# Between a gating layer and a latent-attention layer: how the next norm's sum of squares is formed, and which engine does which piece

## The chip, the core and the metric

The kernel runs on one core of a Trainium2 chip. The metric is the device time of one execution in microseconds (us). Every time inside a profile is counted from the start of the core's span.

## The reference, cut to what matters

Two residual layers and a third block follow one another, for one sequence of 256 tokens with 2048 channels, in float32. Around the change this is computed:

```
x = x + gate * rms_norm(y, post_g)                 # end of layer 0, y = (u * vm * silu(z)) @ sgu_w_out
h = rms_norm(x, pre_g) * (1 + scale) + shift       # start of layer 1 (latent attention)
z = h @ mla_w_in                                   # 2048 -> 3072, first block: 512 columns
rms_norm(a, g) = a * rsqrt(mean(a * a) + 1e-6) * g
```

`gate`, `scale` and `shift` are vectors of 2048 numbers for each layer, made from the condition `c` and the weights `ada_w`. Each norm needs a sum over all 2048 channels of a token before any channel can go on, so at this place the end of one matrix product, two norms in a row and the beginning of the next matrix product form one dependent chain.

## The kernel before, in words

**Tiles.** The 256 tokens are two tiles of 128 (t = 0 and 1), tokens on partitions. Channels are handled in four blocks of 512 (b = 0 to 3) and in eight pairs of 128-channel columns (p = 0 to 7). `x[:, t, :]` is the residual stream, `y[:, t, :]` the output of the mixer and later the normalized input of the next layer.

**Matrix products in three parts.** Each weight and each activation is split into a rounded high part and a low part, and TensorE runs high x high, high x low and low x high. A weight chunk is 128 x 1024 numbers (two groups of 128 input channels by 512 output columns). For every chunk ScalarE makes the high part (`hi_next`, L616 to L631, the copy at L630), VectorE the low part (`lo_next`, the subtraction at L1305), and TensorE uses both. `AHEAD` is 3: the engines make chunk q + 3 at step q, in four slots (`CHUNKS`). `act_steps(n, k)` and `dve_steps(n, k)` are k such steps. A slot comes free when TensorE has used it for both tiles, at `chunk_used`. SyncE loads the raw weights into four slots of two chunks each and waits only for the low part of a chunk four loads back.

**Order.** Every engine has one queue in an order written out by hand; semaphores tie the queues together. Nothing is scheduled at run time, so an instruction that waits holds everything behind it on its engine.

**End of layer 0.** The last product (`sgu_w_out`, second half of its input channels) runs in four blocks. In blocks 0 to 2 TensorE fills a PSUM bank, ScalarE copies it to `stage`, GpSimd adds it to `y`, ScalarE squares `y` with an accumulated sum (`bss`, L959), and GpSimd multiplies `y` by the gate vector `grow` (`gate`, L2302, signals `y_gated`). Beside this VectorE makes weighted sums of `ada_w` (`ada_sum`, L1330) for layer 1. The last four chunks of block 3 are run tile by tile (`pe_by_tiles`, L2543, L2544, L2547): first tile 0 for four chunks (`half_done`), then eight small matmuls (`columns`, L2481), then tile 1.

**The transition, per tile.** ScalarE squares the last block out of PSUM (`act_tile_square`, L770). VectorE adds the four block sums (`dve_tile_ss`, L1484, L1485), multiplies the last block by the gate (`dve_tile_gated`, L1498), ScalarE takes the root (`act_tile_root`, L763), VectorE the reciprocal (`dve_tile_rstd`, L1490). VectorE updates `x` in four blocks (`dve_x_update`, L1503), ScalarE squares each updated block (`act_x_square`, L777), the sums give a second root and reciprocal, and VectorE writes the normalized blocks of `x` to `y` (`dve_x_normal`, L1509), which releases TensorE's transposes.

**Pairs.** `pe_pair` (L2570) transposes a pair of 128-channel columns into one of four PSUM banks. `act_pair` scales and shifts both with the modulation (L791, "modulates") and rounds the result to `a_hi` (L798, "rounds"). `dve_pair` subtracts for `a_lo` (L1533, the "low part" of an activation pair). Pairs 0 to 3 are the first half of the channels of tile 0, pairs 4 to 7 that of tile 1, pairs 8 to 15 the second half of both, tile by tile. In the kernel before, VectorE modulates pairs 2 and 3 (`dve_modulated`, L1517) and ScalarE only rounds them.

**Start of layer 1.** The first block of `mla_w_in` has eight chunks, called M0 to M7 here. M0 to M3 are run for tile 0 and then again for tile 1; tile 0's M0 needs the low part of pair 0, M1 that of pair 1, and so on; tile 1's M0 to M3 need pairs 4 to 7. M4 to M7 are run for both tiles at once and need pairs 8 to 15, two each. Around the first four transposes TensorE has matmuls whose result is not read (`unread`, L2608): six in front of them and five behind.

## Time and profile before

| | |
|---|---|
| median of 3 runs | 2481.65 us (2478.64 to 2482.20) |
| the profiled execution | 2477.93 us |
| its span on the core | 2476.1 us (1.8 us of it lie outside the span) |
| granted TensorE clock, mean | 0.999 of full speed |
| TensorE matmul (PE) busy | 2433.2 us, 98% |
| VectorE (DVE) busy | 1889.0 us, 76% |
| ScalarE (ACT) busy | 1399.4 us, 57% |
| GpSimd (POOL) busy | 442.0 us, 18% |
| instructions | 31108 |

PEld is the weight load of TensorE, which overlaps the matmuls. A row of the timeline gives the start and the length of an instruction or of a merged group, and in brackets how long the engine had sat idle before it and who released it. Lengths include the tail of an instruction: the next one on the same engine can start about 0.08 us before the printed end.

### The profile page before, as it was taken

How to read it: one execution, taken by the hardware profiler on the slowest of the kernel's cores; microseconds unless marked ns; L12 is line 12 of the kernel's file. 1: busy time of each engine (PE TensorE's matmuls, PEld its weight loads, DVE VectorE, ACT ScalarE, POOL GpSimd, SP SyncE). 2: the span in 40 equal slices, each digit the busy share in tenths (PEclk: the TensorE clock that was granted, in tenths of full speed). 3: DMA queues.
4: the chain of work that ended last, by engine and by line, in shares of the span. 5: the costliest groups of instructions: out<-in, count | busy, mean ns of one | idle time of the engine just before them, and what ended most of it. 6: DMA issues, size and time to landing. Idle time of an engine off the chain costs nothing.

```text
span 2476.1 us, 31108 instructions
## 1 busy us (share of the span) xinstructions
PE 2433.2 (98%) x11597; PEld 2018.7 (82%) x11597; DVE 1889.0 (76%) x2295; ACT 1399.4 (57%) x1934; POOL 442.0 (18%) x298
## 2 busy tenths in 40 slices
PE   6999999999999999998999999999999999999999
PEld 5888888888887989887888888888888888888887
DVE  7899798977777787866655555557988878788884
ACT  6655765444447555555566676755655545555553
POOL 0264563111020000110000000043111021111111
PEclk9999999999999999999999999999999999999999
DMA  9999677978784877754555556455465555646454
GB/s 364 321 341 349 237 256 273 336 283 290 271 313 149 246 212 220 233 208 149 167 173 163 177 153 183 157 187 187 155 236 170 204 187 191 217 170 221 170 203 154
DMA packets 370999, 549.47 MB, mean 222 GB/s; under 512 B 31405, under 2 KB 158129, under 8 KB 370225
## 3 DMA queue, kind: packets, MB, share of 16 engines
q1 hardware_dynamic: 368688, 539.54, 64.6%
q10 hardware_dynamic: 1824, 6.04, 0.7%
q0 software_dynamic: 352, 2.11, 0.2%
q8 instruction: 83, 1.36, 0.2%
q14 instruction: 52, 0.42, 0.0%
HBM read 545.53 MB, written 2.11 MB: 221 GB/s over the span
## 4 chain that ended last, share of the span: by engine, by line
PE 88%; DVE 8%; ACT 2%; issue 1%; DMA 1%; SPq 0%; POOL 0%; DVEq 0%; ACTq 0%; POOLq 0%
PE ps L2393 48%; PE ps L2398 24%; DVE lo L1305 3%; PE ps L2423 2%; PE ps L2419 2%; PE ps L2420 2%; DVE ps L1330 1%; PE ps L2379 1%; PE ps L2378 1%; PE ps L2380 1%; DVE lo L1282 1%; DMA raw<-in_sgu_w_in 1%; PE ps L3007 1%; PE ps L2655 1%; ACT hi L630 1%
## 5 line engine op out<-in xcount | busy, mean ns | idle before, releaser
L1305 DVE TENSOR_TENSOR lo<-raw,hi 128x1024 fp32r<-128x1024 f32 x550 | 706.9, 1304 | 350.8 <-ACT hi L630 350.2
L630 ACT ACTIVATE hi<-raw 128x1024 fp32r<-128x1024 f32 x550 | 571.3, 1051 | 431.3 <-PE ps L2398 352.7
L2393 PE MATMUL ps<-hi,a_hi 128*128 128x512 f32 (+1 forms) x2016 | 798.6, 396 | 2.1 <-issue 0.9
L2393 PE MATMUL ps<-hi,a_lo 128*128 128x512 f32 (+1 forms) x2016 | 785.6, 390 | 0.0
L2398 PE MATMUL ps<-lo,a_hi 128*128 128x512 f32 (+1 forms) x2016 | 539.0, 389 | 1.5 <-DVE lo L1305 1.5
L616 ACT ACTIVATE hi<-raw 128x1024 fp32r<-128x1024 f32 x339 | 358.2, 1060 | 292.7 <-PE ps L2398 255.2
L1282 DVE TENSOR_TENSOR lo<-raw,hi 128x1024 fp32r<-128x1024 f32 x339 | 424.4, 1272 | 107.2 <-ACT hi L616 105.0
L2393 PEld LDWEIGHTS ps<-hi,a_hi 128*128 128x128 f32 x2016 | 378.7, 188 | 85.1 <-issue 5.3
L2398 PEld LDWEIGHTS ps<-lo,a_hi 128*128 128x128 f32 x2016 | 378.4, 188 | 81.1 <-DVE lo L1305 1.9
L2393 PEld LDWEIGHTS ps<-hi,a_lo 128*128 128x128 f32 x2016 | 378.9, 188 | 74.4
L2393 PE MATMUL ps<-hi,b_hi 128*128 128x512 f32 x880 | 347.4, 395 | 0.6 <-ACT y L1015 0.3
L2393 PE MATMUL ps<-hi,b_lo 128*128 128x512 f32 x880 | 343.2, 390 | 0.0
L2398 PE MATMUL ps<-lo,b_hi 128*128 128x512 f32 x880 | 235.7, 390 | 0.0
L2227 POOL TENSOR_TENSOR v<-v,stage 128x512 f32<-128x512 f32 (+1 forms) x88 | 146.5, 1665 | 395.8 <-ACT stage L649 371.8
L2398 PEld LDWEIGHTS ps<-lo,b_hi 128*128 128x128 f32 x880 | 165.2, 188 | 35.2
L2393 PEld LDWEIGHTS ps<-hi,b_hi 128*128 128x128 f32 x880 | 165.3, 188 | 34.6 <-issue 0.7
L2393 PEld LDWEIGHTS ps<-hi,b_lo 128*128 128x128 f32 x880 | 165.4, 188 | 33.2
L2227 POOL TENSOR_TENSOR v<-v 128x512 f32<-128x512 f32 x48 | 79.2, 1662 | 589.1 <-ACT v L809 304.7
L1330 DVE SCALAR_TENSOR_TENSOR ps<-raw,cond,ps 128x512 f32<-128x512 f32 x194 | 137.6, 747 | 0.9 <-DMA raw<-in_ada_w 0.8
L2227 POOL TENSOR_TENSOR x<-x,stage 128x512 f32 (+1 forms) x38 | 71.2, 1874 | 332.5 <-DVE stage L1548 310.6
L649 ACT ACTIVATE stage<-ps 128x512 f32<-128x512 f32 x120 | 65.3, 593 | 51.4 <-PE ps L2398 48.2
L1330 DVE SCALAR_TENSOR_TENSOR acc_b<-raw,cond,acc_b 128x512 f32<-128x512 f32 x90 | 72.8, 809 | 0.0
(351 smaller groups left out, 2436.6 us busy)
## 6 DMA issues: line engine op xcount, KB each, us to landing
raw<-in_sgu_w_in SPq DMA_DIRECT2D x88, 1024.0 KB
raw<-in_ada_w SPq DMA_DIRECT2D x64, 1024.0 KB
raw<-in_w_up SPq DMA_DIRECT2D x64, 1024.0 KB
raw<-in_w_down SPq DMA_DIRECT2D x64, 1024.0 KB
raw<-in_w_in SPq DMA_DIRECT2D x42, 1024.0 KB
raw<-in_ada_w SPq DMA_DIRECT2D x64, 512.0 KB
raw<-in_sgu_w_out SPq DMA_DIRECT2D x32, 1024.0 KB
raw<-in_w_in SPq DMA_DIRECT2D x128, 256.0 KB
```

The lines of the kernel that those rows point to most:

```text
L616: nc.scalar.activation(by_rows(hi[:, q % CHUNKS, :]), raw_piece(place), ACT.Copy).then_inc(hi_ready, 1)
L630: nc.scalar.activation(hi[:, q % CHUNKS, 0:width], raw[:, r % RAWS, q % 2 * CW:q % 2 * CW + width], ACT.Copy).then_inc(hi_ready, 1)
L649: nc.scalar.activation(to, ps[:, 2 * s + t, 0:width], func, scale=rstd[:, t:t + 1] if normed else 1.0).then_inc(acc_free, 1)
L1282: nc.vector.tensor_tensor(by_rows(lo[:, q % CHUNKS, :]), raw_piece(place), by_rows(hi[:, q % CHUNKS, :]).bitcast(F32), ALU.subtract).then_ ...
L1305: nc.vector.tensor_tensor(lo[:, q % CHUNKS, 0:width], raw[:, r % RAWS, q % 2 * CW:q % 2 * CW + width], hi[:, q % CHUNKS, 0:width].bitcast( ...
L1330: ins = nc.vector.scalar_tensor_tensor(out=out[:, :] if a == j == 3 else to, in0=w, scalar=c, in1=to, op0=ALU.mult, op1=ALU.add)
L2227: return nc.gpsimd.tensor_tensor(out_, a, b, op)
L2393: nc.tensor.matmul(ps[:, 2 * s + t, 0:width], x[:, k0 + j, t * P:(t + 1) * P], hi[:, c, w], start=begins, stop=False)
L2398: ins = nc.tensor.matmul(ps[:, 2 * s + t, 0:width], x2[0][:, k0 + j, t * P:(t + 1) * P], lo[:, c, w], start=False, stop=last and j == kts - 1)
L2419: nc.tensor.matmul(ps[:, bank, :], left(j)[0], hi[:, c, w], start=begins and j == 0, stop=False)
L2420: nc.tensor.matmul(ps[:, bank, :], left(j)[1], hi[:, c, w], start=False, stop=False)
L2423: ins = nc.tensor.matmul(ps[:, bank, :], left(j)[0], lo[:, c, w], start=False, stop=ends and j == 1)
```

## The change

The sum of squares of the updated `x` is no longer taken from the updated `x`. With r the factor of the gated norm (`rgate`), the new x is x + r*y, so its sum of squares is the old sum + r * (the sum of 2*x*y) + r * r * (the sum of y*y), y being gated. ScalarE sums the squares of gated `y` (`gx[..., 0, b]`) and VectorE the products 2*x*y (`gx[..., 1, b]`), block by block: those of blocks 0 to 2 are placed inside the last product, those of block 3 in the transition. `dve_tile_next` then forms the sum in four small dependent operations, without waiting for the updates of `x`.

In the transition ScalarE normalizes the first two blocks of each tile (`act_x_normal`) and modulates all pairs; VectorE updates two blocks of each tile before the second reciprocal or beside it, and the other four just ahead of pair 4's low part. ScalarE's roundings of the weight chunks and VectorE's low parts stand at other places between them. TensorE's six unread matmuls in front of the transposes are gone; the five behind them stay. The squares of `x` (`act_x_square`) and VectorE's modulation of pairs 2 and 3 are gone here.

The diff, with the declarations of the new buffers and semaphores left out:

```diff
@@ -777,6 +783,26 @@
+        def act_x_normal(act, n, t, b, updated):
+            at = slice(b * NB, (b + 1) * NB)
+            act.wait_ge(n_rstd, n.nrm.base)
+            act.wait_ge(x_updated, updated)
+            nc.scalar.activation(y[:, t, at], x[:, t, at], ACT.Copy, scale=rstd[:, t:t + 1]).then_inc(n_out, 1)
+        def act_gated_square(act, t, b):
+            nc.scalar.activation(gated_parts[:, 2 * b + t, :], y[:, t, b * NB:(b + 1) * NB], ACT.Square,
+                                 accum_out=gx[:, t, 0, b:b + 1]).then_inc(gated_sq, 1)
+        def act_block_gated(act, layer, b):
+            act.wait_ge(y_gated, 6 * layer + 2 * b + 2)
+            if layer:
+                act.wait_ge(gated_sq, 8)
+            for t in range(T):
+                act_gated_square(act, t, b)
@@ -959,35 +985,39 @@
...
                     n.bsq.base += 1
+                if b:
+                    act_block_gated(act, 0, b - 1)
             act_steps(act, n, 2)
             nc.scalar.activation(early[:, :], ones[:, :], ACT.Sqrt)
             act_steps(act, n, 1)
+            act_block_gated(act, 0, 2)
             act.wait_ge(stage_free, n.stg.at(2))
             act.wait_ge(half_done, 1)
             act_tile_square(act, n, 0, 1)
             act_tile_root(act, n, 0)
+            act.wait_ge(acc_free, n.acc.base + 4)
+            act_gated_square(act, 0, 3)
+            act_tile_root(act, n, 0)
+            act_x_normal(act, n, 0, 0, 1)
+            act_x_normal(act, n, 0, 1, 2)
             act_steps(act, n, 1)
-            for b in range(4):
-                act_x_square(act, n, 0, b, b + 1)
+            act.wait_ge(scales, GROUPS + 1)
+            act_pair(act, n, 0, *PAIRS[0], 1)
             act.wait_ge(chunk_used, n.chunk.base + 2 + CHUNKS)
             act_tile_square(act, n, 1, 1)
+            act_tile_root(act, n, 1)
+            act_pair(act, n, 1, *PAIRS[1], 1)
+            act.wait_ge(acc_free, n.acc.base + 6)
+            act_gated_square(act, 1, 3)
             n.acc.base += 2
-            act_tile_root(act, n, 0)
             act_steps(act, n, 1)
+            act_pair(act, n, 2, *PAIRS[2], 1)
             act_tile_root(act, n, 1)
-            act.wait_ge(scales, GROUPS + 1)
-            act_pair(act, n, 0, *PAIRS[0], 1)
-            act_pair(act, n, 1, *PAIRS[1], 1)
-            act_x_square(act, n, 1, 0, 5)
-            act_steps(act, n, 1)
-            act_x_square(act, n, 1, 1, 6)
-            act_pair(act, n, 2, *PAIRS[2], 1, rounds_only=True)
-            act_pair(act, n, 3, *PAIRS[3], 1, rounds_only=True)
-            act_x_square(act, n, 1, 2, 7)
-            act_x_square(act, n, 1, 3, 8)
-            act_steps(act, n, 1)
-            act_tile_root(act, n, 1)
+            act_x_normal(act, n, 1, 0, 3)
+            act_x_normal(act, n, 1, 1, 4)
+            act_pair(act, n, 3, *PAIRS[3], 1)
+            act_steps(act, n, 2)
             for i in range(4, 16):
                 act_pair(act, n, i, *PAIRS[i], 1)
                 if i in (7, 9, 11, 13):
@@ -1484,12 +1514,36 @@
-        def dve_tile_rstd(dve, n, t):
+        def dve_tile_rstd(dve, n, t, to=rstd):
             dve.wait_ge(n_sd, n.nrm.base + 1)
-            nc.vector.reciprocal(rstd[:, t:t + 1], sd[:, t:t + 1]).then_inc(n_rstd, 1)
+            nc.vector.reciprocal(to[:, t:t + 1], sd[:, t:t + 1]).then_inc(n_rstd, 1)
             n.nrm.base += 1
             dve.wait_ge(n_rstd, n.nrm.base)
+        def dve_crossed(dve, t, b):
+            at = slice(b * NB, (b + 1) * NB)
+            nc.vector.scalar_tensor_tensor(out=crossed_parts[:, 2 * b + t, :], in0=x[:, t, at], scalar=2.0, in1=y[:, t, at],
+                                           op0=ALU.mult, op1=ALU.mult, accum_out=gx[:, t, 1, b:b + 1]).then_inc(x_crossed, 1)
+        def dve_block_crossed(dve, layer, b):
+            dve.wait_ge(y_gated, 6 * layer + 2 * b + 2)
+            for t in range(T):
+                dve_crossed(dve, t, b)
+        def dve_tile_next(dve, n, layer, t):
+            one = slice(t, t + 1)
+            dve.wait_ge(x_crossed, 8 * layer + 7 + t)
+            dve.wait_ge(gated_sq, 8 * layer + 7 + t)
+            then(dve, n, nc.vector.tensor_reduce(gsum[:, t, :], gx[:, t, :, :], AX, ALU.add))
+            then(dve, n, nc.vector.scalar_tensor_tensor(out=cross[:, one], in0=gsum[:, t, 0:1], scalar=rgate[:, one], in1=gsum[:, t, 1:2],
+                                                        op0=ALU.mult, op1=ALU.add))
+            then(dve, n, nc.vector.scalar_tensor_tensor(out=xsq[:, one], in0=cross[:, one], scalar=rgate[:, one], in1=xsq[:, one],
+                                                        op0=ALU.mult, op1=ALU.add))
+            nc.vector.tensor_scalar(var[:, one], xsq[:, one], D * EPS, 1.0 / D, ALU.max, ALU.mult).then_inc(n_var, 1)
         def dve_tile_gated(dve, layer, t, s, frees):
@@ -1497,14 +1551,16 @@
             dve.wait_ge(gate_landed, 16 * (layer + 1))
             nc.vector.tensor_tensor(y[:, t, last], ps[:, 2 * s + t, :], grow[:, last], ALU.mult).then_inc(acc_free, frees)
-        def dve_x_update(dve, t, b):
+        def dve_x_update(dve, t, b, factor=rstd):
             at = slice(b * NB, (b + 1) * NB)
-            nc.vector.scalar_tensor_tensor(out=x[:, t, at], in0=y[:, t, at], scalar=rstd[:, t:t + 1], in1=x[:, t, at],
+            nc.vector.scalar_tensor_tensor(out=x[:, t, at], in0=y[:, t, at], scalar=factor[:, t:t + 1], in1=x[:, t, at],
                                            op0=ALU.mult, op1=ALU.add).then_inc(x_updated, 1)
-        def dve_x_normal(dve, t, b):
+        def dve_x_normal(dve, t, b, updated=None):
+            if updated is not None:
+                dve.wait_ge(x_updated, updated)
             at = slice(b * NB, (b + 1) * NB)
             nc.vector.tensor_scalar(y[:, t, at], x[:, t, at], rstd[:, t:t + 1], None, ALU.mult).then_inc(n_out, 1)
@@ -1751,12 +1807,17 @@
                 n.acc.base += 2
                 if b == 1:
                     ada_part(dve, n, 10)
+                if b:
+                    dve_block_crossed(dve, 0, b - 1)
+                else:
+                    then(dve, n, nc.vector.tensor_scalar(xsq[:, :], ss[:, :], D * EPS, None, ALU.add))
             ada_cols(dve, n, 1, 0, 7, 7, 0)
             for k in range(5):
                 lo_next(dve, n)
                 if k in (0, 2):
                     ada_sum(dve, n, 2 + k // 2)
                 n.chunk.base += 1
+            dve_block_crossed(dve, 0, 2)
             ada_keep(dve, n, 1, 28)
...
@@ -1767,50 +1828,42 @@
             dve.wait_ge(block_sq, 2 + n.bsq.base)
             dve_tile_ss(dve, n, 0, bss)
             dve_tile_gated(dve, 0, 0, 1, 2)
+            dve_tile_rstd(dve, n, 0, rgate)
+            dve.wait_ge(acc_free, n.acc.base + 4)
+            dve_crossed(dve, 0, 3)
+            dve_tile_next(dve, n, 0, 0)
+            dve_x_update(dve, 0, 0, rgate)
+            dve_x_update(dve, 0, 1, rgate)
             dve_tile_rstd(dve, n, 0)
-            dve.wait_ge(y_gated, 6)
-            for b in range(4):
-                if b == 3:
-                    dve.wait_ge(acc_free, n.acc.base + 4)
-                dve_x_update(dve, 0, b)
             dve_steps(dve, n, 1)
-            n.sq.base += 4
-            dve.wait_ge(n_ss, n.sq.base)
-            dve_tile_ss(dve, n, 0, xss)
             n.bsq.base += 1
             dve.wait_ge(block_sq, 2 + n.bsq.base)
-            dve_tile_rstd(dve, n, 0)
-            for b in range(2):
-                dve_x_normal(dve, 0, b)
             dve_tile_ss(dve, n, 1, bss)
             dve_tile_gated(dve, 0, 1, 1, 2)
+            dve_pair(dve, n, 0, *PAIRS[0], 1)
+            dve_tile_rstd(dve, n, 1, rgate)
+            dve.wait_ge(acc_free, n.acc.base + 6)
+            dve_crossed(dve, 1, 3)
+            dve_pair(dve, n, 1, *PAIRS[1], 1)
+            dve_steps(dve, n, 1)
+            dve_tile_next(dve, n, 0, 1)
+            dve_x_update(dve, 1, 0, rgate)
+            dve_pair(dve, n, 2, *PAIRS[2], 1)
             dve_tile_rstd(dve, n, 1)
-            dve_x_update(dve, 1, 0)
-            dve_pair(dve, n, 0, *PAIRS[0], 1)
-            dve_x_update(dve, 1, 1)
-            dve_modulated(dve, n, 2, *PAIRS[2], 1, 1)
-            dve_pair(dve, n, 1, *PAIRS[1], 1)
-            dve_modulated(dve, n, 3, *PAIRS[3], 1, 1)
-            dve_steps(dve, n, 1)
-            dve_x_update(dve, 1, 2)
-            dve.wait_ge(acc_free, n.acc.base + 6)
-            dve_x_update(dve, 1, 3)
-            dve_pair(dve, n, 2, *PAIRS[2], 1)
+            dve_x_update(dve, 1, 1, rgate)
             dve_steps(dve, n, 1)
             dve_pair(dve, n, 3, *PAIRS[3], 1)
             n.kept.base += 16
             n.acc.base += 2
             dve_steps(dve, n, 1)
-            n.sq.base += 4
-            dve.wait_ge(n_ss, n.sq.base)
-            dve_tile_ss(dve, n, 1, xss)
-            dve_tile_rstd(dve, n, 1)
-            dve_x_normal(dve, *PIECES[2])
-            dve_x_normal(dve, *PIECES[3])
+            dve_x_update(dve, 0, 2, rgate)
+            dve_x_update(dve, 1, 2, rgate)
+            dve_x_update(dve, 0, 3, rgate)
+            dve_x_update(dve, 1, 3, rgate)
             for i in range(4, 16):
                 dve_pair(dve, n, i, *PAIRS[i], 1)
                 if i in (4, 5, 6, 7):
-                    dve_x_normal(dve, *PIECES[i])
+                    dve_x_normal(dve, *PIECES[i], i + 1)
                 if i in (9, 11, 13):
                     dve_steps(dve, n, 1)
@@ -2685,17 +2738,15 @@
             block_in(0, {3: lambda: pe_ada_parts(pe, n, 4, 7, 7, 0, 11)})
             for c in range(4):
                 pe_chunk(pe, n, A, 1, 2 * c, 2, NB, False, False)
-            pe_by_tiles(pe, n, A, 1, range(8, 16, 2), ends=True, tells=True, before={(1, 0): columns})
-            n.acc.base += 2
             kept0 = n.kept.base
             split0 = n.tg.base
             normal = lambda t, p: 2 + PIECES.index((t, p // 2)) + 1
             pair = lambda i: pe_pair(pe, n, i, *PAIRS[i], normal(*PAIRS[i]), t_kept, kept0)
             split = lambda i: pe.wait_ge(t_lo, split0 + i + 1)
             n.kept.base += 16
+            pe_by_tiles(pe, n, A, 1, range(8, 16, 2), ends=True, tells=True, before={(1, 0): columns})
+            n.acc.base += 2
             pe.wait_ge(acc_free, n.acc.at())
-            unread(0, 6)
             for i in range(4):
                 pair(i)
             unread(0, 5)
```

## Rows read from the trace of the kernel before

**Rows 1.** The page, part 1: busy time and share of the span.

```profile
PE 2433.2 (98%) x11597; PEld 2018.7 (82%) x11597; DVE 1889.0 (76%) x2295; ACT 1399.4 (57%) x1934; POOL 442.0 (18%) x298
```

**Rows 2.** Windows: length, busy (count) of PE, PEld, DVE, ACT, POOL, granted clock, DMA.

```profile
722.00:744.00 22.00, 22.00 (x100) 18.22 (x99) 17.66 (x21) 10.77 (x15) 7.69 (x5) 1.00 0.81 286
764.00:801.00 37.00, 31.79 (x156) 24.16 (x155) 26.24 (x53) 30.38 (x70) 0.00 (x0) 1.00 0.28 78
```

**Rows 3.** Timeline of TensorE: start, length, what, [idle before, released by].

```profile
764.44 1.50 PE L2608 MATMUL ps<-cst 128*128 128x128 f32 x12
766.26 1.09 PE L2570 MATMUL ps<-cst,y 128*128 128x128 f32 x8 [0.32 <-DVE y L1509]
767.19 1.28 PE L2608 MATMUL ps<-cst 128*128 128x128 f32 x10
768.74 0.50 PE L2543 MATMUL ps<-hi,a_hi 128*128 128x512 f32 x1 [0.27 <-DVE a_lo L1533]
...
773.81 0.50 PE L2543 MATMUL ps<-hi,a_hi 128*128 128x512 f32 x1 [0.93 <-DVE a_lo L1533]
...
777.70 0.41 PE L2570 MATMUL ps<-cst,y 128*128 128x128 f32 x2 [2.02 <-issue]
...
779.92 0.50 PE L2543 MATMUL ps<-hi,a_hi 128*128 128x512 f32 x1 [0.19 <-DVE a_lo L1533]
...
800.57 0.36 PE L2393 MATMUL ps<-hi,a_hi 128*128 128x448 f32 x1
```

**Rows 4.** Timeline of VectorE, same columns.

```profile
743.05 1.23 DVE L1305 TENSOR_TENSOR lo<-raw,hi 128x1024 fp32r<-128x1024 f32 x1 [1.73 <-ACT hi L630]
...
759.07 0.16 DVE L1346 COPY mod<-ps 128x4 f32<-128x4 f32 x1 [1.88 <-PE ps L2481]
...
759.85 0.69 DVE L1498 TENSOR_TENSOR y<-ps,v 128x512 f32<-128x512 f32 x1
...
760.64 2.74 DVE L1503 SCALAR_TENSOR_TENSOR x<-y,rstd,x 128x512 f32<-128x512 f32 x4
...
768.26 0.42 DVE L1533 TENSOR_TENSOR a_lo<-tf,a_hi 128x256 fp32r<-128x256 f32 x1
...
773.34 0.42 DVE L1533 TENSOR_TENSOR a_lo<-tf,a_hi 128x256 fp32r<-128x256 f32 x1
...
779.44 0.43 DVE L1533 TENSOR_TENSOR a_lo<-tf,a_hi 128x256 fp32r<-128x256 f32 x1 [1.44 <-ACT a_hi L798]
```

**Rows 5.** Timeline of ScalarE, same columns.

```profile
758.33 0.60 ACT L770 ACTIVATE acc_b<-ps 128x512 bf16<-128x512 f32 x1 [5.05 <-PE ps L2547]
...
760.61 1.06 ACT L630 ACTIVATE hi<-raw 128x1024 fp32r<-128x1024 f32 x1 [0.46 <-PE ps L2547]
...
767.00 0.79 ACT L791 ACTIVATE tf<-ps,mod,hscale 128x128 f32<-128x128 f32 x2
767.82 0.42 ACT L798 ACTIVATE a_hi<-tf 128x256 fp32r<-128x256 f32 x1
...
769.90 1.04 ACT L630 ACTIVATE hi<-raw 128x1024 fp32r<-128x1024 f32 x1
```

**Rows 6.** Groups by line, 757 to 801 us: busy, mean ns of one, idle before.

```profile
L1305 DVE TENSOR_TENSOR lo<-raw,hi 128x1024 fp32r<-128x1024 f32 x12 | 14.4, 1219 | 0.0
L649 ACT ACTIVATE v<-ps 128x512 f32<-128x512 f32 x1 | 0.6, 597 | 0.7 <-PE ps L2398 0.7
L777 ACT ACTIVATION_READ_ACCUMULATOR acc_b<-x 128x1 f32 x8 | 1.5, 186 | 0.0
L763 ACT ACTIVATE sd<-var 128x1 f32<-128x1 f32 x4 | 0.8, 200 | 3.0 <-DVE var L1485 3.0
L1485 DVE TENSOR_SCALAR var<-ss 128x1 f32<-128x1 f32 x4 | 0.6, 154 | 0.1
```

**Rows 7.** Windows at the next transition, columns as in rows 2.

```profile
1124.70:1127.76 3.06, 1.10 (x9) 0.86 (x8) 2.49 (x11) 2.44 (x8) 0.00 (x0) 1.00 0.00 0
1127.76:1134.58 6.82, 3.53 (x17) 3.46 (x17) 6.75 (x18) 6.15 (x16) 0.00 (x0) 0.50 0.02 3
```

More of the change, by code:

```diff
@@ L314, in build @@
         xss = sb("xss", [P, T, 4])
+        gx = sb("gx", [P, T, 2, 4])
+        gsum = sb("gsum", [P, T, 2])
+        xsq, rgate, cross = (sb(k, [P, T]) for k in ("xsq", "rgate", "cross"))
         early = sb("early", [P, 1])
@@ L371, in build @@
         turned_x = tf[:, :, :].rearrange("p a (b e s) -> p (a b) e s", b=2, e=2)
+        gated_parts = v[:, 0, D:2 * D].bitcast(BF16).rearrange("p (k n) -> p k n", k=8)
+        crossed_parts = v[:, 1, :].rearrange("p (k n) -> p k n", k=8)
         junk = stage[:, :, :].rearrange("p t n -> p (t n)").bitcast(BF16)
@@ L417, in build @@
         block_sq, gate_kept, y_gated = sem("block_sq"), sem("gate_kept"), sem("y_gated")
+        gated_sq, x_crossed = sem("gated_sq"), sem("x_crossed")
         gate_written, gate_landed = sem("gate_written"), sem("gate_landed")
```

## The prediction

> **What bounds the kernel now.** I read the page's busy shares first: TensorE is busy 98% of the span [rows 1], so time can only be won or lost where TensorE stands idle or does work that nobody needs. Then the windows. In the last product of layer 0 TensorE is busy in all of 22 us; in the transition, 764 to 801 us, it is busy 31.8 of 37, some of that with unread matmuls, while ScalarE is busy 30.4 [rows 2]. Here the order of ScalarE's and VectorE's queues sets the time. TensorE's timeline shows the holes one by one [rows 3]: unread matmuls from 764.44, transposes at 766.26, the first real chunk (M0, tile 0) at 768.74, M2 at 773.81 after 0.93 us idle, pair 4's transposes at 777.70 after 2.02 us idle, tile 1's M0 at 779.92, and the next block at 800.57. From 764.44 that is 36.1 us. Nothing else of the kernel is touched, and behind this stage TensorE is the bound again, so the shift of 800.57 is the shift of the whole time, if nothing gives it back.
>
> **How the sum is made.** I walk through the three queues in their new order. An instruction starts when the one before it lets go, or when what it waits for has come, plus 0.05 to 0.1 us. Lengths: product, update of 512 columns 0.75 each and 0.67 from start to start (four take 2.74 us) [rows 4]; weight chunk's low part 1.22 [rows 6], 1.14 from start to start; its rounding on ScalarE 1.05, 0.96 from start to start; modulate and round one pair 0.79 + 0.42, in all 1.15 until ScalarE is free [rows 5]; square 0.60 [rows 5] plus 0.19 to read the accumulator, overlapping to 0.7; copy of 512 columns 0.60, root 0.20, a small VectorE operation 0.15, 0.19 when the next depends on it [rows 6]; pair's low part 0.42, gate product 0.69 [rows 4]. The old order walked in the same way reaches the next block 0.2 us later than the trace, so I trust differences to some 0.5 us.
>
> **Inside the last product.** Twelve instructions are new: six squares on ScalarE (0.7 us each), six products on VectorE. I cost them at nothing. Those of blocks 0 and 1 fall beside idle time such as the 1.73 us in front of VectorE's low part at 743.05 [rows 4]. The products of block 2 come at 757.2, where VectorE sits idle 1.88 us until 759.07 [rows 4], and the squares into ScalarE's 5.05 idle us before 758.33 [rows 5]. If that cover were gone, tile 0's chain would start later by the excess.
>
> **The product with an accumulated sum** is in no row of VectorE. Lower bound: the update, the same operation and shape without the sum, 0.75 [rows 4]. Upper bound: the nearest longer row, 1.22, a low part of twice the columns [rows 6]. I take 0.94: the update plus ScalarE's 0.19 for reading an accumulator, the nearest row to that step [rows 6]. Walked with 0.75 the shift of the end is 3.3 us, with 0.94 3.5, with 1.22 4.1. The Trainium skill (Vector Engine (DVE) Microarchitecture Reference, section 7, Points that are easy to get wrong) says that this instruction with two SBUF sources other than bf16 runs at half throughput, with no port left for reading the accumulator. The update without the sum, two f32 sources, takes 0.75 [rows 4]; no row here has the sum with it, so the trace can't bear the rule out. By it the product would take twice the update, about 1.4 us, and the shift would be 4.6.
>
> **Tile 0's chain.** Unchanged up to the gate product, which ends at 760.54 [rows 4]. Then product to 761.6, four small operations to 762.4, root, and meanwhile two updates to 763.6; reciprocal to 763.8; ScalarE normalizes block 0 from 763.9 to 764.5. The old chain released the transposes at 766.26; now they start at 764.5, and the six unread matmuls (1.50 us [rows 3]) are gone. That is 1.7 us won. But ScalarE now has behind it: normalize block 1 to 765.0, round M0 (old at 760.61 [rows 5]) to 766.0, modulate and round pair 0 to 767.1, where the old one ended at 768.24. VectorE can't take pair 0's low part yet: tile 1's sum and gate product stand ahead of it, and they wait for ScalarE's square of tile 1 (767.0 to 767.7). So the low part starts at 768.65 (old: 768.26 [rows 4]) and M0 at 769.1 against 768.74. **The win is spent: +0.4.**
>
> **Tile 1's chain.** ScalarE: pair 1 to 769.5, square of gated y to 770.1, round M1 to 771.2. VectorE's low part of M1 ends at 772.4, about as before. Then four small operations to 773.0, update to 773.7, pair 2's low part from 773.7 (old 773.34), reciprocal to 774.2. TensorE could start M2 at 774.1. But M2's rounding, old at 769.90 [rows 5], now stands behind two normalizations (774.2 to 775.6, the second waiting for its update) and pair 3 (to 776.7): it ends at 777.7. **TensorE starts M2 at 777.8 against 773.81 [rows 3]: +4.0, after some 4.8 us idle.** That is what is late next.
>
> **What comes back, and goes again.** The old 2.02 us in front of pair 4 go, since block 0 of tile 1 is normalized by then: M3 starts only 1.5 us late. But VectorE has behind M2: its low part to 779.0, pair 3's, M3's low part to 780.4, and then four updates, 2.7 us, all in front of pair 4's low part, which starts at 783.1 against 779.44 [rows 4]. Tile 1's M0 starts at 783.5 against 779.92 [rows 3], or against 780.08 in the walk of the old order: **+3.5.** From there both orders alternate pair by pair in the same way, ScalarE giving the pace, and the shift stays to the end of the block: 804.1 against 800.57. No DMA is added, and the DMA engines are busy 0.28 of this stage [rows 2], so I add nothing for loads.
>
> On the profiled execution's own 2477.93 us (span 2476.1) this gives 2481.4. That execution stands 3.7 us under the median of 2481.65; on the median I forecast 2481.65 + 3.5 = **2485.2 us**. A measurement of this kernel can tell about 0.2%, 5.0 us, from no change, so this is a forecast of "within 0.2%", on the slow side.
>
> **Rival 1, slower by more than 0.2%: the clock falls in the new hole.** At the next transition TensorE was busy 1.10 us of 3.06, and then the granted clock went from 1.00 to 0.50 (2.4 to 1.2 GHz) for 6.82 us [rows 7]. In the old transition at 764 it stayed at 1.00 [rows 2], but there the longest hole was 2.02 us, and now there are 4.8 us before M2 and 2.4 before tile 1's M0. Against: a fall in the first hole costs nothing if the clock is back by 783, since TensorE waits there for VectorE anyway. It decides if low clock still holds when tile 1's chunks begin. Slowing TensorE's pieces by 1.85 in the walk for 3.4 to 6.8 us from 779 to 784 adds 0.7 to 2.1 us; with 2.1 the time is 2487.3, +0.23%. The Trainium skill (TensorE: Matmul & The Clock Gate, What's actually happening) says that the default is the throttled clock and that activity releases it, which agrees with rows 7.
>
> **Rival 2: the accumulated product is dear** (the upper bound and above): 2485.7 to 2486.3, a wait of VectorE in tile 0's chain.
>
> **Rival 3: TensorE isn't held at M2.** If the 4.8 us don't appear (ScalarE reaches M2's rounding by 774, through a quicker chain than the rows give), the four updates ahead of pair 4 are left and the walk ends 2.1 us after the old one (2483.8); with them overlapped too it is 0.2 (2481.9). If the 1.7 us won at the transposes and the 2.02 us at pair 4 stayed won in full, it would be 2478. For it: both really are released earlier. Against: seven pieces of ScalarE, each with a row, stand in front of M2's rounding. That the change doesn't do what its title says is part of the forecast: the four updates stand in one lump in front of pair 4's low part, so the low parts aren't even there.
>
> **Chances.** Forecast as walked 0.54; rival 1 0.18; rival 2 0.10; rival 3 0.18. Slower by over 0.2% gets most of rival 1, a third of rival 2 and, since medians of three vary by 1 to 2 us, some 0.10 of the forecast: 0.27. Faster by over 0.2% needs 2476.7: a third of rival 3 at most, 0.06. The rest, 0.67, is within 0.2%. The range takes in rival 1 with noise above (2488.8) and most of rival 3 below (2479.5).
>
> **What would show it.** Right: transposes at about 764.5; M0 near 769; one hole of 4 to 5 us before M2, released by ScalarE's L630; no hole at pair 4; four updates in a row before pair 4's low part; a hole of about 2.4 us before tile 1's M0; next block at about 804; products of 0.75 to 0.94 us. Wrong: M2 starting before 775, a granted clock of 0.5 inside 765 to 800, products of 1.2 us or more, or waits for DMA in the block.

## The result, and the profile after

The changed kernel takes 2483.41 us (median of 22 runs, 2481.24 to 2487.49) against 2481.57 for the kernel before on the same chip (22 runs): the ratio is 1.0012, 95% interval 1.0006 to 1.0017. By the ratio it is slower by 3.0 us (1.5 to 4.2); the two medians themselves differ by 1.84 us. Either is within the 0.2% that counted as no change. The profiled execution took 2483.45 us, span 2481.6. TensorE's share is the same as in [rows 1]. Part 1 of the page:

```profile
PE 2435.2 (98%) x11585; PEld 2019.5 (81%) x11585; DVE 1891.1 (76%) x2308; ACT 1403.0 (57%) x1942; POOL 441.9 (18%) x298
```

The two spans differ by 5.5 us, more than the ratio says: the profiled execution of the kernel before, 2477.93 us, was faster than each of its 22 runs (lowest 2478.64). To see where, I measure one stage in every kernel of this study: from the start of the eight small matmuls that make the modulation of the layer (TensorE's last work before the gate of the last block can be applied) to the first 448-column matmul of the next block. Before, this **stage** goes from 758.08 to 800.57; after, from 759.85 to 806.01. So 1.77 us arise ahead of it, and **3.67 us in it**; nothing is left for the rest of the kernel. The stage is a steadier measure than the whole time: in the changed kernel and the six variants of it that keep the order up to there (experiments 1, 2, 3, 5, 9 and 10), tile 0's M0 starts 10.98 to 11.00 us into it. What does vary from one execution to the next is the clock, as experiment 12 shows. Windows over the stage and over the stretch with a low clock in it, columns as in [rows 2], before first:

```profile
758.08:800.57 42.49, 37.28 (x184) 28.81 (x183) 30.61 (x63) 34.33 (x79) 0.00 (x0) 1.00 0.33 97
```

The same of the kernel after:

```profile
759.85:806.01 46.16, 37.61 (x172) 28.92 (x171) 30.26 (x65) 34.76 (x75) 0.00 (x0) 0.93 0.30 92
777.00:783.83 6.83, 4.12 (x11) 3.27 (x12) 4.24 (x6) 4.24 (x8) 0.00 (x0) 0.52 0.24 78
```

No engine has noticeably more to do than before. TensorE stands idle 8.6 us of the stage (46.16 less 37.61), where it was 5.2. TensorE's timeline after shows where; it answers to [rows 3], with every start 1.8 us late from what came ahead of the stage:

```profile
766.32 1.18 PE L2623 MATMUL ps<-cst,y 128*128 128x128 f32 x8
767.34 1.28 PE L2661 MATMUL ps<-cst 128*128 128x128 f32 x10
...
770.84 0.50 PE L2596 MATMUL ps<-hi,a_hi 128*128 128x512 f32 x1 [2.22 <-DVE a_lo L1589]
...
779.71 0.77 PE L2596 MATMUL ps<-hi,a_hi 128*128 128x512 f32 x1 [4.88 <-ACT hi L636]
...
785.33 0.50 PE L2596 MATMUL ps<-hi,a_hi 128*128 128x512 f32 x1 [0.16 <-DVE a_lo L1589]
...
806.01 0.36 PE L2446 MATMUL ps<-hi,a_hi 128*128 128x448 f32 x1
```

M2 is at 779.71, behind a hole of 4.88 us that ScalarE's rounding ended. At pair 4 there is no hole any more. The granted clock was 0.50 from 777.2 to 784.1, so it fell inside the hole; in M2's own row the length is 0.77 where M0 took 0.50. VectorE's timeline, answering to [rows 4]:

```profile
758.90 0.69 DVE L1527 SCALAR_TENSOR_TENSOR v<-x,y 128x512 f32<-128x512 f32 x1
759.51 0.08 DVE L1527 DVE_READ_ACCUMULATOR v<-x,y 128x1 f32 x1
760.84 0.16 DVE L1376 COPY mod<-ps 128x4 f32<-128x4 f32 x1 [0.63 <-PE ps L2534]
...
763.37 0.22 DVE L1542 SCALAR_TENSOR_TENSOR cross<-gsum,rgate 128x1 f32<-128x1 f32 x1
...
770.37 0.41 DVE L1589 TENSOR_TENSOR a_lo<-tf,a_hi 128x256 fp32r<-128x256 f32 x1
...
779.59 1.23 DVE L1335 TENSOR_TENSOR lo<-raw,hi 128x1024 fp32r<-128x1024 f32 x1 [2.94 <-ACT hi L636]
...
782.21 2.73 DVE L1557 SCALAR_TENSOR_TENSOR x<-y,rgate,x 128x512 f32<-128x512 f32 x4
784.86 0.41 DVE L1589 TENSOR_TENSOR a_lo<-tf,a_hi 128x256 fp32r<-128x256 f32 x1
```

Pair 0's low part at 770.37 releases M0 at 770.84. VectorE sits idle 2.94 us for the same rounding as TensorE, and does its four updates in one lump after it; pair 4's low part comes at 784.86, and that releases tile 1's M0 at 785.33. ScalarE's timeline, answering to [rows 5]:

```profile
775.90 1.57 ACT L791 ACTIVATE y<-x,rstd 128x512 f32<-128x512 f32 x2 [0.86 <-DVE rstd L1520]
777.38 0.79 ACT L817 ACTIVATE tf<-ps,mod,hscale 128x128 f32<-128x128 f32 x2
...
778.52 1.99 ACT L636 ACTIVATE hi<-raw 128x1024 fp32r<-128x1024 f32 x2
```

These are tile 1's two normalizations, pair 3's modulation, and then the roundings of M2 and M3 back to back. The groups by line, 759 to 807 us, answer to [rows 6]:

```profile
L791 ACT ACTIVATE y<-x,rstd 128x512 f32<-128x512 f32 x4 | 2.8, 718 | 2.2 <-DVE rstd L1520 2.1
L1527 DVE SCALAR_TENSOR_TENSOR v<-x,y 128x512 f32<-128x512 f32 x4 | 2.7, 690 | 0.1
L1527 DVE DVE_READ_ACCUMULATOR v<-x,y 128x1 f32 x4 | 0.3, 84 | 0.0
```

The product with an accumulated sum takes 0.69 us and 0.08 for reading the accumulator; ScalarE's normalization takes 0.72.

### The profile page after: what moved, and what is told of

It reads as the page before. It is cut to its first block, busy times and chain, and to the rows that moved or that the text cites. A ratio compares the mean times of both kernels' runs of the same rounds, so it can differ in the third digit from the quotient of the medians.

```text
span 2481.6 us, 31102 instructions
## 1 busy us (share of the span) xinstructions
PE 2435.2 (98%) x11585; PEld 2019.5 (81%) x11585; DVE 1891.1 (76%) x2308; ACT 1403.0 (57%) x1942; POOL 441.9 (18%) x298
## 4 chain that ended last, share of the span: by engine, by line
PE 87%; DVE 7%; ACT 2%; issue 1%; DMA 1%; SPq 0%; POOL 0%; ACTq 0%; DVEq 0%; POOLq 0%
PE ps L2446 48%; PE ps L2451 24%; DVE lo L1335 2%; PE ps L2476 2%; PE ps L2473 2%; PE ps L2472 2%; DVE ps L1360 1%; DMA raw<-in_sgu_w_in 1%; PE ps L2432 1%; PE ps L2431 1%; PE ps L2433 1%; DVE lo L1312 1%; ACT hi L636 1%; PE ps L3058 1%; PE ps L2708 1%
```

## The experiments

**Theory A:** the order of two queues costs the 3.7 us. M2's rounding stands behind the normalizations and pair 3 on ScalarE, and four updates stand in a lump ahead of pair 4's low part on VectorE. **Rivals:** B, the twelve operations added inside the last product delay the stage; C, the clock that falls in the new hole costs it. Whole times scatter (31 runs of the kernel before on two other chips lie between 2478.7 and 2486.7 us), so the verdicts go by the stage, of one profiled execution each; each whole time stands with that of the kernel before on the same chip. Experiments 1 to 6, 9 and 10 have one run each, and so has the kernel before beside 1 to 4. To see what a move wins apart from a later fall of the clock, I also use the start of **tile 1's M0**, counted from the start of the stage: 21.84 us before the change, 25.48 after it. From there to the end of the stage it is 20.6 to 20.7 us in both, and in every variant with the old order behind it in which the clock holds from there on. In the runs' code the loops over pairs 4 to 15 are written out and the semaphore counts passed along; the extracts show what changes place.

**1. M2's rounding early.** Only one step of ScalarE moves:

```
 act_pair(act, n, 2, *PAIRS[2], 1)
+act_steps(act, n, 1)
 act_tile_root(act, n, 1)
...
 act_pair(act, n, 3, *PAIRS[3], 1)
-act_steps(act, n, 2)
+act_steps(act, n, 1)
```

> The changed kernel with one piece moved on ScalarE: the rounding of weight chunk M2 stands right behind pair 2 instead of behind the two normalizations of tile 1 and pair 3. Measure: the stage from the start of the eight small matmuls (ps<-ones,acc x8) to the first 448-column matmul, 42.49 us before the change and 46.16 after it. Theory A (the order of the two queues holds TensorE, first at M2's rounding, then at the four updates): M2 starts 3.6 to 3.9 us earlier, the hole of 4.88 us before it shrinks to about 1, but M3 waits for its own rounding, so the stage gets 1.5 us shorter, 44.7. Theory B (the added work and ScalarE's sum of work make the stage longer, whatever its order): the stage stays within 0.5 us of 46.16. Theory C (the low TensorE clock in the hole costs the time): the clock doesn't fall and the stage gets shorter by the 1.5 to 3 us that slow matmuls cost, whatever the updates do.

Measured: stage 45.30 us (763.00 to 808.30), whole 2485.76 against 2482.4. It wins 0.9 of the 3.7, less than A's 1.5. The clock was low twice, from 774.7 to 778.1 and from 788.3 to 791.7. The stage and the second low stretch, and tile 1's M0:

```profile
763.00:808.30 45.30, 38.72 (x172) 29.61 (x171) 30.21 (x65) 34.73 (x75) 0.00 (x0) 0.92 0.31 92
788.50:791.50 3.00, 3.00 (x10) 2.46 (x9) 0.82 (x2) 2.11 (x6) 0.00 (x0) 0.50 0.00 1
```

```profile
787.02 0.50 PE L2623 MATMUL ps<-hi,a_hi 128*128 128x512 f32 x1 [2.04 <-DVE a_lo L1603]
```

Tile 1's M0 is at 24.02 us (787.02 less 763.00), 1.46 earlier than in the changed kernel: that is A's 1.5. In the second low stretch, behind it, TensorE is busy all 3.00 us, so it is the bound there, and 0.6 us of the win are lost again.

**2. The updates spread.** Only VectorE's four updates move:

```
-dve_x_update(dve, 0, 2, rgate)
-dve_x_update(dve, 1, 2, rgate)
-dve_x_update(dve, 0, 3, rgate)
-dve_x_update(dve, 1, 3, rgate)
 dve_pair(dve, n, 4, *PAIRS[4], 1)
+dve_x_update(dve, 0, 2, rgate)
 dve_x_normal(dve, 0, 2, 5)
 dve_pair(dve, n, 5, *PAIRS[5], 1)
+dve_x_update(dve, 1, 2, rgate)
...
```

> The changed kernel with the four updates of x that stood in one lump in front of pair 4's low part now standing one by one behind the low parts of pairs 4, 5, 6 and 7, each just ahead of the normalization that needs it; ScalarE as in the changed kernel. Theory A: the hole before M2 stays at 4.9 us, pair 4's low part comes 1.8 us earlier or more, and the stage gets 1.8 us shorter, 44.4 us against 46.16. Theory B: within 0.5 us of 46.16. Theory C: the clock falls as in the changed kernel and the stage stays at 46.16.

Measured: stage 46.34 us, whole 2484.92 against 2482.4. By itself this is a miss for A. The stage's windows:

```profile
761.07:807.41 46.34, 39.16 (x171) 30.29 (x170) 30.54 (x65) 34.75 (x75) 0.00 (x0) 0.89 0.29 89
780.00:786.50 6.50, 5.58 (x14) 4.34 (x15) 3.63 (x5) 2.94 (x5) 0.00 (x0) 0.50 0.26 66
```

The clock was low from 779.9 to 786.7 here as well, but now pair 4's low part is early, and TensorE has chunks to do in that stretch: busy 5.58 of 6.50 us. Tile 1's M0 starts only when they are done, at 25.71 us (786.78 less 761.07), without a wait:

```profile
786.78 0.48 PE L2622 MATMUL ps<-hi,a_hi 128*128 128x512 f32 x1
```

Experiment 10 tests this reading.

**3. Both moves.** Edits 1 and 2 together.

> Both moves together: M2's rounding behind pair 2, and the updates spread. Theory A: 3.8 us shorter than the changed kernel, 42.3 us, which is what the stage took before the change (42.49), so the whole loss is these two places. Theory B: 45.7 us or more. Theory C: about 44 us, as with the first move alone.

Measured: whole 2481.70 against 2482.4, and the stage:

```profile
761.87:804.25 42.38, 37.33 (x172) 28.12 (x171) 30.58 (x65) 34.62 (x75) 0.00 (x0) 0.96 0.33 97
```

```profile
783.60 0.47 PE L2623 MATMUL ps<-hi,a_hi 128*128 128x512 f32 x1
```

42.38 us against 42.49 before the change, and tile 1's M0 is at 21.73 us (783.60 less 761.87) against 21.84. **The whole loss is back, by order alone**, with every added operation kept, though the clock was low in this run too, from 774.1 to 777.5, ahead of M2.

**4. The added operations alone.** The kernel before, with the squares and products inside the last product; nothing uses their sums:

```
 act_steps(act, n, 1)
+act_block_gated(act, 0, 2)
...
+dve_block_crossed(dve, 0, 2)
```

> The kernel before, with only the twelve added operations inside the last product (six squares of gated y on ScalarE, six products 2xy on VectorE); their sums are not used and the transition is the old one. Theory A: they are hidden; the three blocks in front take the same time as before (22.0 us for a block) and the stage is 42.5 us, within 0.2. Theory B: the block or the stage is longer by 1 us or more, since products of two SBUF tiles delay VectorE's low parts and tile 0's first sum.

Measured: stage 42.54 us, whole 2481.04 against 2482.4. Windows of the product and of the stage:

```profile
694.00:738.00 44.00, 44.00 (x196) 36.43 (x196) 37.83 (x41) 22.62 (x32) 12.21 (x8) 1.00 0.83 288
760.99:803.53 42.54, 37.32 (x183) 28.79 (x182) 30.93 (x65) 34.39 (x79) 0.00 (x0) 1.00 0.32 97
```

With the added work TensorE is busy in all of 44.00 us, though VectorE is busy in 37.83 of them. B falls.

**5. The hole filled.** Thirty unread matmuls ahead of M2, to hold the clock:

```
-(0, 2): lambda: (split(2),),
+(0, 2): lambda: (unread(1, 30), split(2),),
```

> The changed kernel with 30 matmuls of 128 columns whose result is not read, into a free PSUM bank, in TensorE's hole before M2, so that TensorE is not idle there. Theory A: the granted clock stays at 1.00 from 765 to 800 us, M2 and M3 run at full speed, but tile 1's M0 still waits for pair 4's low part behind the four updates: the stage stays at 46.2 us, within 0.3. Theory C (the low clock costs the time): the stage gets 1.5 us shorter or more.

Measured: stage 46.53 us (A said 46.2 within 0.3), whole 2486.04 against 2481.38. The clock had fallen at 774.2 already and was back at 777.6, ahead of the filling, so C wasn't tested as meant. But the run shows another thing, in TensorE's timeline and in the window over the filling:

```profile
777.79 6.86 PE L2687 MATMUL ps<-cst 128*128 128x128 f32 x60
784.41 0.47 PE L2622 MATMUL ps<-hi,a_hi 128*128 128x512 f32 x1
...
788.07 0.50 PE L2622 MATMUL ps<-hi,a_hi 128*128 128x512 f32 x1 [0.19 <-DVE a_lo L1602]
```

```profile
777.79:784.41 6.62, 6.62 (x61) 6.61 (x60) 3.65 (x6) 4.45 (x7) 0.00 (x0) 1.00 0.41 138
```

The filling, all of it at a clock of 1.00, is longer than the hole and holds M2 until 784.41. From the stage's start that is 2.4 us later than in the changed kernel, and the stage is only 0.37 us longer. Tile 1's M0 again waits for VectorE's low part; that came 0.4 us later since pair 4's transposes stand behind M2, and VectorE waited 0.34 us for ScalarE's rounding of the pair. So M2's own start isn't what sets the end: the rounding is, through VectorE, which waits for it ahead of the low parts and the four updates.

**6. The six unread matmuls.** The change took them out. Here the kernel before, without them:

```
-unread(0, 6)
```

> The kernel before with nothing changed but the six unread matmuls in front of the first transposes left out. Theory A: the transposes waited for the normalized x anyway (they were free at 765.94 and started at 766.26), so the stage stays at 42.5 us within 0.2, unless the clock falls. Rival: the six stood on the path and the stage gets up to 1.5 us shorter.

Measured: whole 2482.50 against 2481.38, and the stage:

```profile
761.46:805.08 43.62, 37.23 (x171) 28.40 (x170) 30.61 (x63) 34.32 (x79) 0.00 (x0) 0.96 0.31 95
782.30:785.50 3.20, 3.20 (x10) 2.45 (x9) 1.16 (x3) 1.67 (x5) 0.00 (x0) 0.50 0.56 214
```

```profile
781.07 0.41 PE L2570 MATMUL ps<-cst,y 128*128 128x128 f32 x2 [2.02 <-issue]
```

1.13 us longer than with them, all of it in a stretch with the clock low, 782.1 to 785.5, where TensorE is busy throughout. Up to pair 4's transposes nothing moved: they are at 19.61 us (781.07 less 761.46) against 19.62. So the six are off the path by themselves. Whether they hold the clock isn't shown: the fall came some 13 us behind the place where they stood, each kernel has one profile here, and experiment 12 shows a fall coming and going in one and the same kernel. The two executions with the six that have a profile, the kernel before and experiment 4, had none in the stage.

**7. The three queues reordered.** The changed arithmetic in a new order. ScalarE: two roundings (M0, M1) ahead of tile 0's root; M2's rounding right behind that root; block 1 of tile 0 normalized after pair 0; M3's rounding ahead of tile 1's normalizations. VectorE: low parts of M0 and M1 earlier, tile 0's updates 1 and 2 ahead of tile 1's gate, only one update left ahead of pair 4. TensorE: transposes of pairs 4 to 7 ahead of tile 0's M3. ScalarE's part of the diff:

```
+act_steps(act, n, 2)
...
-act_x_normal(act, n, 0, 0, 1)
-act_x_normal(act, n, 0, 1, 2)
+act_x_normal(act, 0, 0, 1, r0 + 2)
+act.wait_ge(chunk_used, m0 + 3 + CHUNKS)
+act_tile_square(act, n, 1, 1)
...
+act_x_normal(act, 0, 1, 2, r0 + 2)
...
-act_x_normal(act, n, 1, 0, 3)
-act_x_normal(act, n, 1, 1, 4)
...
+act_steps(act, n, 1)
+act_x_normal(act, 1, 0, 4, r0 + 4)
+act_x_normal(act, 1, 1, 5, r0 + 4)
```

> The changed kernel with the same pieces on the same engines, but ScalarE's, VectorE's and TensorE's queues of the transition in another order: the roundings of M0, M1 and M2 stand ahead of or between the first normalizations, tile 0's updates and low parts of weights fill VectorE's waits, the updates of blocks 2 and 3 are spread up to pair 7, and TensorE's transposes of pairs 5 to 15 stand one to three places earlier. Theory A, by the walk through the three queues: the stage takes 36.7 to 37.5 us against 46.16 after and 42.49 before, and the whole kernel is about 5 us faster than before (ratio 0.998) and 8 us faster than after. Theory B: no better than before, 42 us or more.

Measured: 2474.52 us (7 runs, 2471.8 to 2476.45) against 2481.38 (13 runs), ratio 0.9969 (0.9958 to 0.998). Its stage's window, and from the timeline the only two holes from the first transposes to the end of the stage:

```profile
758.03:794.46 36.43, 34.08 (x172) 27.40 (x170) 29.75 (x65) 34.02 (x75) 0.00 (x0) 1.00 0.38 114
```

```profile
765.14 0.63 PE L2649 MATMUL ps<-cst,y 128*128 128x128 f32 x4 [0.55 <-ACT y L791]
...
767.57 0.66 PE L2649 MATMUL ps<-cst,y 128*128 128x128 f32 x4 [1.80 <-ACT y L791]
```

The stage is 6.1 us shorter than before the change, and the whole 6.9 by medians. **This version beats both kernels:** its ratio to the kernel before is 0.9969, that of the changed kernel 1.0012.

**8. The same, normalized on VectorE.** Does it matter that ScalarE normalizes? The first two blocks of each tile go to VectorE, with the order adapted:

```
-act_x_normal(act, 0, 0, 1, r0 + 2)
-act_x_normal(act, 0, 1, 2, r0 + 2)
...
+dve_x_normal(dve, 0, 0, 1)
+dve_x_normal(dve, 0, 1, 2)
```

> As the reordered kernel, but VectorE writes the four first normalized blocks (0.48 us each, as before the change) and ScalarE does not; queues ordered anew for that. Theory A: by the walk the stage takes 37.1 to 37.9 us, about the same as with ScalarE normalizing, 5 us faster in all than before. A rival (what is saved on ScalarE pays twice, since ScalarE is the busiest engine of the stage): under 36.5 us.

Measured: 2474.87 us (7 runs), ratio 0.9969 (0.9958 to 0.998); stage 36.65. Not told apart from experiment 7: once the order fits, it makes no difference that these runs show which engine normalizes.

**9. and 10. The clock, by a pair.** The same filling in two kernels: 14 unread matmuls in place of five behind the first transposes, 19 ahead of M2. In 9 in the changed kernel, in 10 in the kernel of experiment 2:

```
-unread(0, 5)
+unread(0, 14)
...
-(0, 2): lambda: (split(2),),
+(0, 2): lambda: (unread(1, 19), split(2),),
```

> The changed kernel with TensorE kept busy: fourteen unread matmuls instead of five behind the first transposes (about 2.0 us more, the hole before M0 was 2.2), and nineteen before M2 (about 4.2 us; the hole was 4.9). The one with thirty before M2 was longer than its hole and came too late for a clock that had fallen at 774. Theory A: the granted clock stays at 1.00 through the stage and the stage takes 46.2 us, within 0.3, since VectorE's pair 4 is what tile 1 waits for and slow matmuls had room in front of it. Theory C (the low clock was part of the change's loss): 45.5 us or less.

> The same unread matmuls in the kernel with the updates spread, which took 46.34 us instead of the 44.4 walked, with a clock of 0.50 from 779.8 to 786.7 us. If the low clock ate the gain, the stage takes 44.2 to 44.7 us now, with a clock of 1.00. If spreading the updates is worth nothing (TensorE or ScalarE would have waited for something else), it stays at 46 us or more.

Measured: 9 has 2489.73 us and stage 47.13, 10 has 2481.28 us and stage 44.44, against 2481.14. Windows of 9, then of 10:

```profile
765.23:812.36 47.13, 43.37 (x228) 34.94 (x226) 30.13 (x65) 34.77 (x75) 0.00 (x0) 0.96 0.29 88
791.50:794.50 3.00, 3.00 (x10) 2.41 (x10) 0.30 (x1) 0.82 (x3) 0.00 (x0) 0.50 0.14 53
```

```profile
759.47:803.91 44.44, 42.04 (x228) 33.76 (x226) 30.55 (x65) 34.76 (x75) 0.00 (x0) 1.00 0.31 93
```

In 10 the clock held at 1.00, and the stage is 1.9 us shorter than in experiment 2 (46.34): the low clock was what hid A's gain there, and with it out of the way spreading the updates is worth 46.16 less 44.44, 1.7 us. Tile 1's M0 says the same, at 23.79 us (783.26 less 759.47) against 25.48 in the changed kernel and 25.71 in experiment 2:

```profile
783.26 0.50 PE L2622 MATMUL ps<-hi,a_hi 128*128 128x512 f32 x1 [0.21 <-DVE a_lo L1602]
```

In 9 the clock held through M2 and fell later (791.3 to 794.7), in a stretch where TensorE is busy throughout. Two rows of its TensorE timeline:

```profile
785.10 0.47 PE L2622 MATMUL ps<-hi,a_hi 128*128 128x512 f32 x1 [0.64 <-ACT hi L636]
...
790.73 0.50 PE L2622 MATMUL ps<-hi,a_hi 128*128 128x512 f32 x1 [1.90 <-DVE a_lo L1602]
```

From the stage's start these are M2 at 19.9 and tile 1's M0 at 25.5 us. In the changed kernel they are at 19.9 (779.71 less 759.85) and 25.5 too, with the clock low between them. So the fall at M2 cost it nothing up to there, and C falls for its profiled execution. The stage of 9 still got 1.0 us longer (A said 46.2 within 0.3): from tile 1's M0 to the end it took 21.6 us instead of 20.7, and the later fall lies there.

**11. The old arithmetic reordered.** What is the new sum worth, apart from the order? The kernel before with its queues rearranged in the manner of 7, ScalarE modulating every pair, the six unread matmuls gone; an extract:

```
-dve_modulated(dve, n, 2, *PAIRS[2], 1, 1)
...
-act_pair(act, n, 2, *PAIRS[2], 1, rounds_only=True)
+act_pair(act, n, 2, *PAIRS[2], 1)
```

> The kernel before with its own arithmetic (ScalarE squares the updated x, VectorE normalizes), only its three queues in an order found by the same walk, ScalarE modulating pairs 2 and 3, and the six unread matmuls gone. Walk: 38.2 us for the stage with 0.5 of error, against 42.49 before and 36.43 in the reordered kernel with the new sum of squares; as a whole about 4 us faster than before (ratio 0.998). Theory A: so the order alone is worth 4 us, and the new sum of squares 1 to 2 us more once the order lets it. Rival (the new sum is what makes the reordering possible): 41 us or more.

**12. Experiment 7 again,** beside it.

> The reordered kernel of e7 once more, on the same chip as e11, to compare the two: 36.4 us for the stage and a ratio to before of 0.9958 to 0.998; e11's ratio should lie 0.0005 to 0.001 above it.

Measured: 11 has 2476.27 us (9 runs), ratio 0.9979 (0.9969 to 0.9989), stage 39.84; 12 has 2476.46 us (10 runs), ratio 0.9975 (0.9965 to 0.9984), stage 37.89. The stages are 1.6 and 1.5 us longer than expected, with a clock fall in each. Windows of 11, then of 12:

```profile
760.62:800.46 39.84, 37.07 (x172) 29.68 (x170) 29.21 (x59) 35.32 (x83) 0.00 (x0) 0.91 0.34 105
```

```profile
760.25:798.14 37.89, 35.53 (x171) 28.84 (x170) 29.67 (x65) 34.14 (x75) 0.00 (x0) 0.95 0.35 109
770.50:773.50 3.00, 3.00 (x13) 2.81 (x13) 2.62 (x10) 2.92 (x9) 0.00 (x0) 0.50 0.40 153
```

12 is the kernel of 7, and its stage is 1.46 us longer. TensorE's busy time is 1.45 longer too (35.53 against 34.08), and the clock was low from 770.3 to 773.7, where 7 had none of it. That is the price of one fall on the path, in one and the same kernel. As whole times 11 and 12 aren't told apart; their stages differ by 1.95 us in favour of the new sum, with a clock fall in both, of 3.4 us in 12 and 6.8 in 11. What the new sum is worth by itself stays open, between nothing and about 2 us; most of the gain of either is order (in 11 with the six unread matmuls gone and ScalarE modulating every pair).

## Why the prediction was right

The forecast was +3.5 us and "within 0.2%, on the slow side". Measured are +3.67 in the stage, +3.0 (1.5 to 4.2) as a ratio of whole times, and 2483.41 us, inside the range. The forecast time itself, 2485.2, lies 1.8 us above that. Step by step, with 1.8 us taken off the times after for what came ahead of the stage:

- **Inside the last product: nothing.** Right. Experiment 4 has it alone: 42.54 against 42.49.
- **Transposes at 764.5.** Measured 764.5. **M0 at 769.1.** Measured 769.0. The win of 1.7 us at the transposes was spent in the places named.
- **M2 at 777.8 after a hole of 4.8 us.** Measured 777.9 and 4.88, ended by the rounding named.
- **The hole at pair 4 goes, four updates stand ahead of pair 4's low part at 783.1, tile 1's M0 at 783.5.** Measured 783.1 and 783.5. Experiment 3 shows that this lump and the late rounding are the whole loss.
- **Next block at 804.1.** Measured 804.2. From tile 1's M0 on it took 20.65 us before and 20.68 after, so the shift stayed as walked.
- **The product with the sum, 0.94.** Mis-sized: 0.69 + 0.08 = 0.77, close to its lower bound of 0.75. Rival 2 falls with it. The Trainium skill (Vector Engine (DVE) Microarchitecture Reference, section 7, Points that are easy to get wrong) has half throughput for two SBUF sources other than bf16. That isn't borne out: the 512 columns took 0.69 us, no longer than an update without the sum (four take 2.73), and no more for a column than a low part, also of two f32 sources in SBUF, with 1.23 for 1024.
- **ScalarE's normalization, 0.60.** Mis-sized: 0.72. The row I took it from reads PSUM and has no factor for each token, and this one reads SBUF and has one. The source alone doesn't make the difference: the squares of `x` in the kernel before (L777), out of SBUF without such a factor, took 0.62. The small operations of VectorE with two tensors took 0.22, not 0.15. These and the product's 0.17 too much went against each other in the walk, so part of the closeness at each station is luck.
- **A hole of 2.4 us before tile 1's M0.** Not there as idle time: 0.16 us. The clock had fallen at 777.2, in the hole before M2, and until 784.1 TensorE did M2 and M3 slowly, which filled the time in which it would have waited for VectorE anyway. In experiment 9, with the clock held, that hole is 1.90 us.

**Rival 1** was half right. Its mechanism came (the clock fell to 0.50 in the new hole), and with it one of my own signs of being wrong, a granted clock of 0.5 inside 765 to 800. Its condition, low clock while tile 1's chunks run, wasn't met in the profiled execution: the clock was back at 784.1, and tile 1's M0 started at 785.33. But I had it too narrow: I looked only for one fall at the largest hole. Experiments 1, 2, 3, 5, 6, 9, 11 and 12 show falls at several places of the stage. Some cost nothing that shows, as in experiment 3; those that a comparison could price where TensorE is the bound (1, 2, 6, 9, 12) cost 0.6 to 1.9 us. How much falls cost the changed kernel in its 22 runs isn't known, since only one execution has a profile. That low clock takes more of its runs is on record: the mean granted clock over a run is 0.996 to 0.998 in all 22 (0.997 in the profiled one), while the profiled execution of the kernel before had 0.999, and so had 11 of its 31 runs beside experiments 5 to 12, on other chips. **Rival 3** falls with the measured hole at M2. That the unread matmuls cost nothing to lose was my silent assumption; experiment 6 bears it out up to pair 4 and leaves open whether the fall behind it, 1.1 us, is theirs.

The 1.77 us ahead of the stage belong to no step. The stage starts between 758.0 and 765.2 us in the kernels of this study, with nearly the same work ahead; experiment 6, which has none of the added operations, starts at 761.46. In the two profiles, 0.43 us of the 1.77 arise before TensorE's first transposes (20.02 and 20.45) and 0.88 as longer idle time between 100 and 200 us, far ahead of any changed instruction, with a clock of 1.00 in both. The cause stays open.

## What to carry to other kernels

Where two engines feed a third through queues in program order, walk all queues through the new order, and look for the instruction that several engines wait for: here one rounding, four places too late on ScalarE, and four updates in a lump on VectorE cost 3.8 us together (experiment 3), more than the 1.7 that the shorter chain had won. A change of arithmetic that shortens a chain deserves a new order of its own before it is judged: the same operations gave a ratio of 1.0012 in one order and 0.9969 and 0.9975 in another. Before taking out matmuls whose result nobody reads, or putting some in, look at the granted clock in more than one profile: the same filling left it at 1.00 in experiment 10 and didn't in 9.

## What the runs showed of the hardware

- The granted clock fell to 0.50 also in stretches where the longest hole was far below 4.8 us: in experiment 12 after holes of 0.55 and 1.80 us, and in experiment 7, the same kernel with the same two holes, not at all. One profile does not tell whether a kernel is free of it.
- A fall is free as far as TensorE would wait anyway (changed kernel, 777.2 to 784.1), and costs its full slowing where it is the bound: 1.46 us for 3.4 us of low clock in experiment 12. In the changed kernel the clock came back at 784.1, when TensorE had been busy from 779.7 on. That agrees with the Trainium skill (TensorE: Matmul & The Clock Gate, What's actually happening), by which activity releases it.
- VectorE reads an accumulated sum in 0.08 us, ScalarE in 0.19 [rows 6].
- An unread f32 matmul of 128 columns takes about 0.23 us as two records of the profile (60 records in 6.86 us in experiment 5, and 12 in 1.50 [rows 3], both at a clock of 1.00).
